# Sparse attention: the division by the sums moved from VectorE into the transposing product, by a diagonal that GpSimd makes

## What is computed

```python
s = jnp.einsum('bqhd,bqkd->bqhk', qb, kg) * scale
p = jax.nn.softmax(jnp.where(ok, s, -jnp.inf), axis=-1)
return jnp.einsum('bqhk,bqkd->bqhd', p, vg)
```

## Time and profile before

| | |
|---|---|
| time, three runs | 1426.87 us median (1426.66 to 1427.4) |
| profiled execution, span | 1425.5 us |
| PE busy | 1395.1 us (98%) |
| PE weight loads | 1086.6 us (76%) |
| DVE busy | 711.1 us (50%) |
| ACT busy | 265.9 us (19%) |
| POOL busy | 29.9 us (2%), 32 instructions |
| moved from memory | 426.03 MB |

### The profile page before, as it was taken

The page is one execution under the profiler, slowest core; times in us unless marked ns, Lnnn a source line. Parts: engine busy times, 40 slices in busy tenths (PEclk is TensorE's granted clock), DMA queues, the critical chain, the costliest instruction groups (busy, mean ns, idle before and its releaser), DMA issues.

```text
span 1425.5 us, 39151 instructions
## 1 busy us (share of the span) xinstructions
PE 1395.1 (98%) x18039; PEld 1086.6 (76%) x18039; DVE 711.1 (50%) x1434; ACT 265.9 (19%) x442; POOL 29.9 (2%) x32
## 2 busy tenths in 40 slices
PE   8999999999998899999999999999999999999998
PEld 6868999999887796676676676676676677677675
DVE  7935744547787754443443433533533533433436
ACT  3434544344354221000000000000000000000001
POOL 0000000000001200000000000000000000000000
PEclk9999999999999999999999999999999999999999
DMA  9153655456310169999999999999999999999995
GB/s 308 58 179 105 251 187 201 141 174 215 110 60 3 47 217 382 391 413 414 395 411 415 395 408 414 396 399 411 401 399 409 404 406 409 410 388 412 413 399 211
DMA packets 117258, 433.41 MB, mean 304 GB/s; under 512 B 10171, under 2 KB 13477, under 8 KB 109798
## 3 DMA queue, kind: packets, MB, share of 16 engines
q1 hardware_dynamic: 112768, 420.60, 75.8%
q10 hardware_dynamic: 2966, 5.45, 1.1%
q0 software_dynamic: 1360, 4.85, 1.0%
HBM read 426.03 MB, written 4.85 MB: 302 GB/s over the span
## 4 chain that ended last, share of the span: by engine, by line
PE 90%; DVE 5%; DMA 2%; ACT 1%; issue 1%; SPq 1%; DVEq 0%
PE bank L2943 36%; PE bank L2948 23%; PE bank L2415 5%; PE bank L2414 5%; PE bank L2413 5%; PE bank L2141 2%; DMA ring<-in_moe_w_gate 2%; PE bank L2532 1%; PE bank L2158 1%; PE bank L2317 1%; PE bank L2308 1%; PE bank L2756 1%; PE bank L2393 0%; PE bank L2285 0%; DMA ring<-in_e_w_in 0%
## 5 line engine op out<-in xcount | busy, mean ns | idle before, releaser
L2943 PE MATMUL bank<-ring,yT 128*32 128x384 f32 x5760 | 626.3, 487 | 1.6 <-DMA ring<-in_moe_w_gate 1.3
L2948 PE MATMUL bank<-ring,yT 128*32 128x256 f32 (+1 forms) x3264 | 627.0, 354 | 0.0
L2948 PEld LDWEIGHTS bank<-ring,yT 128*32 128x32 f32 x3264 | 356.5, 110 | 134.3
L2943 PEld LDWEIGHTS bank<-ring,yT 128*32 128x32 f32 x5760 | 228.6, 109 | 45.0 <-issue 9.7
L2948 PE MATMUL bank<-ring,arena 128*32 128x256 f32 x1152 | 252.6, 379 | 0.0
L2943 PE MATMUL bank<-ring,arena 128*32 128x384 f32 x2304 | 252.1, 486 | 0.0
L1988 DVE STREAM_TRANSPOSE arena<-arena 32x256 f32<-32x256 f32 x288 | 189.1, 657 | 109.1 <-PE bank L2948 105.2
L2040 DVE TENSOR_TENSOR arena<-arena,bank 128x384 f32<-128x384 f32 (+1 forms) x56 | 32.1, 609 | 371.5 <-PE bank L2948 232.1
L2415 PE MATMUL bank<-arena_r,ring_r 128*128 128x256 f32 (+1 forms) x672 | 188.5, 280 | 0.0
L2948 PEld LDWEIGHTS bank<-ring,arena 128*32 128x32 f32 x1152 | 126.5, 110 | 60.1
L1110 ACT ACTIVATE arena<-bank 128x384 f32<-128x384 f32 (+1 forms) x56 | 27.4, 534 | 691.3 <-PE bank L2948 468.2
(11 more groups left out here) (487 smaller groups left out, 1217.3 us busy)
## 6 DMA issues: line engine op xcount, KB each, us to landing
ring<-in_moe_w_gate SPq DMA_DIRECT2D x56, 2048.0 KB, 21.7
ring<-in_moe_w_up SPq DMA_DIRECT2D x56, 2048.0 KB, 21.8
ring<-in_moe_w_down SPq DMA_DIRECT2D x56, 2048.0 KB, 19.4
ring<-in_ffn_w_gate SPq DMA_DIRECT2D x5, 2048.0 KB, 7.7
ring<-in_ffn_w_up SPq DMA_DIRECT2D x5, 2048.0 KB, 7.7
ring<-in_ffn_w_down SPq DMA_DIRECT2D x5, 2048.0 KB, 7.9
ring<-in_o_w_in SPq DMA_DIRECT2D x5, 2048.0 KB, 8.0
ring<-in_e_w_in SPq DMA_DIRECT2D x3, 2048.0 KB, 14.7
```

The costliest lines, as they stand in the source:

```text
L2943: pe_.matmul(bank[b + i][QUAD[m], 0:FM], x(m), w[:, FB * i:FB * i + FM], start=start, stop=stop, skip_group_check=True)
L2948: last = pe_.matmul(bank[b + i][QUAD[3], o:o + n * P].rearrange("p (i n) -> p i n", i=n), x(m), side, start=start and o == 0, stop=stop, s ...
```

## The change

Three things.

1. In the odd layer DVE no longer multiplies the exponentials. `sum_inverse(w)` takes only the reciprocal of the two sums and tells POOL by `sums_turned`. POOL multiplies the identity matrix by each of the two columns of reciprocals, which gives two diagonal matrices of 128x128 in a region at the end of the arena (two buffers), and gives `p_ready`. PE, in place of the transpose of a block of exponentials, makes an ordinary product of the block with the diagonal: transposed and divided at once. The first layer keeps its `normalise` and its transposes.
2. POOL's loop over the units stands ahead of its wait for `tilde_done`. It waits also for `into_h` (long reached), and from unit 2 on for the transposes of unit u-2, whose diagonal it overwrites. DVE waits from unit 2 on, before it overwrites a reciprocal, for POOL to have read it.
3. In the RWKV part the semaphore `y0_done` goes: both of its places count `U0_done`, and the one who waits, PE, waits for the higher count. Nothing else of the computation changes.

```diff
+    diag = arena[:, ARENA - 4 * P:ARENA].rearrange("p (b j n) -> p b j n", b=2, j=2)
...
         pl.memset(pre["Bz"], 0.0).then_inc(step("s5_zero")[0], 1)
+
+        pool.wait_ge(sem("into_h"), 8)
+        for u in range(UNITS):
+            pool.wait_ge(sem("sums_turned"), u + 1)
+            if u >= 2:
+                pool.wait_ge(sem("pt_done"), UNITS + u - 1)
+            for j in range(2):
+                s_ = 24 + 2 * (u % 2) + j
+                last = pl.tensor_scalar(diag[:, u % 2, j, :], C("ident"), stat[:, s_:s_ + 1], None, MUL)
+            last.then_inc(sem("p_ready"), 1)
 
         pool.wait_ge(*step("tilde_done"))
...
+        def sum_inverse(w):
+
+            s = 2 * (w % 2)
+            dve.wait_ge(sem("exp_done"), UNITS + w + 1)
+            if w >= 2:
+                dve.wait_ge(sem("p_ready"), UNITS + w - 1)
+            v.reciprocal(stat[:, 24 + s:26 + s], stat[:, 16 + s:18 + s]).then_inc(sem("sums_turned"), 1)
...
             if u:
-                normalise(u - 1, UNITS, p0)
+                sum_inverse(u - 1)
             behind_scores(u)
...
-                        last = pe_.transpose(bank[7][:, o:o + P], p_[:, w % 2, j, kt * P:kt * P + P], ident)
+                        if base:
+                            last = pe_.matmul(bank[7][:, o:o + P], p_[:, w % 2, j, kt * P:kt * P + P], diag[:, w % 2, j, :],
+                                              start=True, stop=True)
+                        else:
+                            last = pe_.transpose(bank[7][:, o:o + P], p_[:, w % 2, j, kt * P:kt * P + P], ident)
...
-            last.then_inc(sem("y0_done"), 1)
+            last.then_inc(sem("U0_done"), 1)
...
-                    pe.wait_ge(sem("U0_done"), t + 1)
-                    pe.wait_ge(sem("y0_done"), t + 1)
+                    pe.wait_ge(sem("U0_done"), 2 * t + 2)
```

More of the change, by code:

```diff
@@ L347, in trunk @@
     L1, end = carve(arena, 0, L1_LAYOUT)
-    assert end <= ARENA, end
+    assert end <= ARENA - 4 * P, end
     assert sum(w for _, w in L1_LAYOUT[:[n for n, _ in L1_LAYOUT].index("lnw")]) <= XLO_ODD
```

## The result

| | before | after |
|---|---|---|
| time, median | 1427.13 us (1426.66 to 1430.55) | 1439.79 us (1438.84 to 1442.51) |
| profiled span | 1425.5 us | 1438.3 us |

A forecast was written before the change was run, and what follows sets the result against it. Bound taken in the odd layer's sparse attention: DVE first, PE from 428.11 us. DVE savings, POOL's multiplies and waits left a 3.5 us slip, the product taken as nothing: 1426.87 + 3.5 = 1430.4 us, range 1426.3 to 1433.2.

The forecast's parts named there:

- What bounds the kernel: Odd layer's sparse attention, about 400 to 441 us: DVE bounds to 428.11, then PE; 256-key units by reciprocal to transposes.
- The 1.4 us around the span stay: Whole run: profiled span 1425.5 us against median 1426.87; the difference stays, so the slip is added to the median.
- Removed from DVE: Normalising multiplies in seven odd-layer units: 0.47 or 0.61 us saved each, 3.7 us in all, only partly winnable.
- Added on POOL: Two 128x128 multiplies per odd-layer unit, 0.3 us each (bounds 0.2 and 0.6), plus 0.1 us per hand-over.
- POOL beside DVE: Behind the odd layer's scores: each POOL multiply waits for a whole two-SBUF-input DVE instruction, taking turns; total slip 3.5 us.
- DVE always first: Rival, unit 7: queued DVE instructions go before waiting POOL, 1.2 us more, about 1431.8; chance 0.26 together with the clock.
- the forecast's turns: Units 2, 4, 7: DVE instruction, POOL multiply, DVE instruction, POOL multiply; slips against before 0.16, 1.3 and 3.5 us.
- DVE's L1532 and L1656 are 0.3 longer: Sign of a right forecast: in units 2 and 4 these DVE instructions take 0.3 us longer, held by POOL's multiply.
- PE idles 1.8 us ahead of unit 4's transposes: Sign of a right forecast: PE, free at 424.9, waits 1.8 us for p_ready, forecast at 426.74.
- The product: PE in the odd layer: a plain f32 product, 0.13 us, replaces a transpose, 0.16 us; cost taken as nothing.
- The rival with a chance of 0.03: Slow product on PE: 22 products cost 0.33 us more each, 7 us; 1434, or 1437 with the waits; chance 0.03.
- The clock: Rival: PE's idle time at 425 to 427 brings half clock, 1.4 us more, about 1431.8; chance 0.26 together with order.

The follow-up runs named there:

- b2_before: The kernel before, run again unchanged for a second trace; ratio to before 0.9998.
- a2: The changed kernel, run again unchanged for a second trace; 1439.52 us, ratio to before 1.0073.
- e15: The kernel before with 48 more PE instructions (12 two-column products in iteration 2 of the odd layer) and nothing else; ratio to before 1.0038.
- e3: The kernel before without the odd layer's multiplies; division left out, ScalarE's copy multiplies by 1/32 instead; ratio to before 0.9995.
- e11: The changed kernel with POOL's two multiplies joined into one two-input multiply that makes both diagonals; ratio to before 1.0037.
- e10: The changed kernel, but in units 4 and 7 DVE waits for its own end between two back-to-back instructions; 1439.99 us, ratio to before 1.0085.
- e14: The changed kernel with one two-input POOL multiply for both diagonals, PE's transposes put back and the division left out; ratio to before 1.0001.
- e2: The changed kernel with PE's transposes put back, still waiting for POOL's two multiplies; division left out (constant 1/32); ratio to before 1.0066.
- e1: The kernel before, with only the odd layer's transposes replaced by ordinary f32 products with the identity; ratio to before 1.0039.
- e8: The changed kernel with four and six keep-warm products on PE ahead of its wait for p_ready in units 4 and 7; ratio to before 1.0055.
- e9: The changed kernel with nine instead of three keep-warm products on PE behind the last expert, ahead of the branch; ratio to before 1.0087.
- e7: No diagonal: ScalarE multiplies the exponentials by the reciprocals in place, PE transposes as in the kernel before, count merged as in the change; ratio to before 1.0002.
- e5: The changed kernel, but DVE instead of POOL makes the diagonals, behind its reciprocal; ratio to before 1.0022.
- e6: The changed kernel, but ScalarE instead of POOL makes the diagonals, ahead of its exponentials; ratio to before 1.0024.
- e13: e7 with two keep-warm products on PE ahead of unit 7's wait; 1427.0 us, ratio to before 0.9992.

## Why the prediction was wrong

*What bounds the kernel.* Right for the stretch: DVE up to unit 4, and from there the way from reciprocal to transposes. "Behind the stretch a slip passes to the end one for one" held for what lies between (99.26 against 99.45, and the experts within 1.8 us in all traces). "The 1.4 us around the span stay" did no harm, but the 1.4 was the median of one set of executions less the span of another: the profiled execution of after took 1440.15 us with a span of 1438.3, that of b2_before 1426.78 with 1425.0, so 1.8 us lie around either. What was missed lies between the two: I never looked at the last 12 us, which grew by 2.6 (a2 against b2) to 3.8 (after against before) on their own. One trace of e15 has the same with PE code that computes nothing new.

*Removed from DVE.* "3.7 us of DVE work", of which at most 0.7 to be won: e3 gave 1.4 in the stretch. The 0.7 was too low, by little; with 1.4 the forecast would have been further off.

*Added on POOL.* This is the term that was mis-sized most. "I take 0.3": it is 0.60. I had the row of 0.63 for 256 columns of two inputs and halved it for half the columns. The halving was wrong: 128x128 with one input takes as long as 128x256 with two (e11). My own sum had 6.5 us for 0.6 a multiply, so the size of this term alone takes the forecast from 3.5 to about 6.5. The 0.1 us for a hand-over, for which I had given no row, held: in unit 4 the reciprocal ends at 423.92 and POOL starts at 424.01.

*POOL beside DVE.* That POOL waits for DVE's two-input instructions was right, the turns were not. "POOL's first multiply sits behind a whole DVE instruction, and its second behind another if they take turns": in unit 2 it looks so (0.97 and 0.85, where DVE waits for its own result between L1549 and L1551). Where DVE's instructions follow back to back, a multiply that arrives during one ends 0.39 us after the next one: behind both in unit 4 (2.55, and the second behind none), behind the second and the fourth in unit 7 (1.48 and 1.32). With a gap after the first it gets in there: 2.55 became 1.50 in e10. The rival "DVE always first" had the order right for unit 4, and in unit 7 only in part, since the first multiply got in after two of the four.

By the forecast's turns p_ready came 1.8, 3.1 and 2.0 us after the reciprocal in units 2, 4 and 7; with 0.6 us a multiply they would give 2.4, 3.7 and 2.6. Measured are 2.05, 3.38 and 3.04. So the turns were too dear in two places and too cheap in one.

"DVE's L1532 and L1656 are 0.3 longer" was wrong for after: 0.48 for one of the two L1532, 1.22 for L1656, as before; the most that DVE lost to a multiply by a column is 0.10 (L1692, 0.78 for 0.68). It is not wrong for every POOL instruction: beside the two-input one of e11 and e14 DVE lost 0.23 to 0.42.

The Trainium skill (SBUF — State Buffer, Who interferes with whom) has the one that issues first take the ports for its whole instruction and the other blocked. The trace agrees in that POOL waited, and in e11 in that DVE did (0.42 of POOL's 0.61 us). It does not agree for POOL's multiply by a column, which took 0.60 and held DVE for 0.10 or less.

"PE idles 1.8 us ahead of unit 4's transposes" came true, 1.83, by luck: counted from the start of the stretch, p_ready and the moment at which PE was free were both some 1.2 us later than forecast. The slips by which I counted show how it grew: DVE takes the scores 0.78 us later than before in unit 3 (forecast 0.16), 1.13 in unit 4 (0.19), 2.85 in unit 5 (1.3), 4.90 in unit 7 (2.3), and in iteration 7 PE transposes 7.12 later (3.5).

All in all, POOL with its two instructions is 5.1 us of stretch alone (e2, less its fall), and with one it is nothing (e14).

*The product.* "Taken as nothing": it costs 2.0 us alone (e1), 2.8 beside POOL (45.05 against 42.22). What failed is the reading of the earlier trace rows: "16 products take 2.05, 0.13 each". The x16 are instructions, and a product of two f32 operands is two matmuls and two weight loads, so these were 8 products of 0.26. A transpose is one instruction, 0.16. The count shows it (24 matmuls more for 24 products), and the row was in my hands: L2606 makes eight products a unit by the code. The rival with a chance of 0.03 had the right mechanism and a price of 0.33 each, 7 us, for which the runs show a third.

The Trainium skill (TensorE: Matmul & The Clock Gate, Terms) gives the transpose mode as four times faster for FP32; the trace does not agree: four take 0.66 us as transposes and 1.16 as products, under twice.

*The clock.* Priced at 1.4 us, and in the range as a rival of 0.26: it is 2.2 to 3.2 (e8 against after and a2). It comes behind the idle time of unit 7 (440.8 to 447.6) and, in a2 and e9, also behind that of unit 4 (430.0 to 433.4 in a2), the sign that I had named. That the fall of the earlier trace rows does not come in every execution, I had not seen.

*"The merged count: nothing".* No run tells it by itself; e7 and e14 carry it and are level with before.

Put together, by differences of traces without a fall of the clock where there is one:

| step | forecast, us | measured, us | by |
|---|---|---|---|
| product for transpose | 0 | 2.0 to 2.8 | e1, e11 - e14 |
| POOL's way, one instruction | | 0 | e14 |
| two instructions for one | | 5.3 | e8 - e11 |
| all of POOL, division off DVE | 3.5 | 5.3 | |
| clock in the stretch | 0 (rival 1.4) | 2.2 to 3.2 | after, a2 - e8 |
| the end | 0 | 2.6 to 3.8 | after, a2 - before, b2 |

The terms give 12.1 to 15.1 against a before without a fall; after's excess over b2_before's span is 13.3. So the steps that failed are two sizes, POOL's multiply (0.3 us taken, 0.60 measured; all of POOL 5.3 us of stretch for 3.5) and the product (taken as nothing, 2.0 to 2.8 us), and two things left out of the forecast, the clock (2.2 to 3.2) and the end (2.6 to 3.8). What stays open is the end. That after, a2, e1, e5, e11 and e15 have 15.0 to 16.0 suggests that it hangs on PE's code, but e6 and e10 have the same 48 instructions more and 13.1 and 12.9, where the kernels without them have 12.0 to 13.3. What sets it is not shown. Nor is e10's time.

## What to carry to other kernels

Count the instructions that an operation becomes, not the calls in the code: the xN of a row shows them, and here it hid a factor of two. Do not scale a small GpSimd operation down from a larger one: here half the columns and one input less saved nothing (0.60 against 0.61 us). It waits for VectorE's two-input instructions, and can miss a turn where they follow without a gap; give it one instruction, not two, or give the work to ScalarE. Look at the last microseconds of the trace too, which the change did not touch and which grew. And count the falls of the clock in a trace before you compare it with another: one of 3.4 us was worth 1.1 us here, as much as several of the effects that were looked for.

## What the runs showed of the hardware

- POOL: a multiply by a column takes 0.60 us for 128x128 (units 1 and 5), the two-input one 0.61 for 128x256 (e11) and 1.04 for 128x512. ACT: 0.40 for 128x128 (e6) and 0.50 for 128x256 (e13). DVE: 0.33 for 128x128 (e5).
- A POOL multiply by a column that arrives during a DVE instruction of two SBUF inputs, with another right behind it, ended 0.39 us after the second (unit 4, both multiplies of unit 7); with a gap of 0.03 us between them, 0.47 after the first (e10). DVE lost 0.10 us or less by it (L1551 0.48, L1675 1.22, L1692 0.78 for 0.68).
- A two-input POOL multiply of 128x256 got in after the first without a gap (1.51 us for 2.55), and the DVE instruction behind was 0.23 to 0.42 us longer (e11, e14).
- An f32 product is two weight loads and two matmuls, 1.16 us for four of 128 columns; a transpose is one of each, 0.66 for four.
- With PE idle for 3.2 us (after, unit 7) the granted clock was then 0.50 for 6.8 us; ahead of the fall in before PE was busy 1.99 of 3.5 us, and in b2_before, busy 2.01 of the same 3.5, none followed. The falls of a stretch cost 1.1 us (3.4 us at the lower level, before) to 3.2 us (10.2 us, a2).
- One branch of PE past a loop took 3.39 to 5.61 us, in eighteen traces; what sets it is not shown.
